# A hybrid transformer step on one core: splitting the experts' weight tiles in halves of 1024 columns

## The chip, the cores and the metric

The kernel runs on one core of a Trainium2 chip. The metric is the time of one execution on the device in microseconds (us). The engines are TensorE (PE, matmuls; its weight loads are shown apart as PEld), VectorE (DVE), ScalarE (ACT), GpSimd (POOL) and SyncE (SP), whose queue issues nearly all loads here. Each engine runs its own list of instructions; they are held together by semaphores, counters that an instruction raises as it ends and on which another waits.

## The reference

Two token sets (256 prompt tokens and 8 x 4 sample tokens, model width 1024) go through two layers: the first has a sparse attention mixer and a dense feed-forward, the second a short convolution and a mixture of 8 experts, of which every token uses 2. All weights are fp32. The change is in the experts:

```python
def _moe(h, w_router, b_router, w_gu, w_down):
    logits = (h @ w_router).astype(jnp.float32) + b_router.astype(jnp.float32)
    top_v, top_i = lax.top_k(logits, TOP_K)
    top_w = jax.nn.softmax(top_v, axis=-1)
    combine = jnp.sum(jax.nn.one_hot(top_i, N_EXPERTS, dtype=jnp.float32) * top_w[..., None], axis=-2).astype(h.dtype)
    out = jnp.zeros_like(h)
    for e in range(N_EXPERTS):
        out = out + combine[..., e:e + 1] * _swiglu(h, w_gu[e], w_down[e])
    return out
```

`_swiglu` is `(silu(h @ w_gate) * (h @ w_up)) @ w_down` with a hidden width of 3584.

## The kernel before

All weights and cache pages stream through one ring of six slots in SBUF (`ring`, 128 partitions x 2048 columns of fp32, 1 MB each). SP issues the loads in the order of use. Before it loads tile n it waits until the tile six places earlier is used (`s_used`, L491 and, in the experts, L505).

Matmuls with fp32 weights of the ada, dense, conv and expert stages are done in three fast matmuls. ACT copies a tile into a buffer of type fp32r, which rounds it (`whi` in the experts, L757), DVE subtracts this high part from the tile (`wlo`, L1307), and PE multiplies high by high, low by high and high by low. Three semaphores carry a tile through. ACT raises `s_split_hi`. DVE waits for that, and raises `s_used`, which frees the ring slot and at the same time tells PE that both parts are there. PE raises `s_tile_done` with its last matmul on the tile, and ACT waits for that before it overwrites the split buffer. The experts have three split buffers (`SPLIT`), so ACT may copy tile i when PE is done with tile i-3.

The expert loop runs eight times on each engine (`experts`, L502 on SP, L751 on ACT, L1297 on DVE, L1796 on PE), for one expert each. Further rounds for over 128 tokens at one expert are in the code, and weren't entered here. An expert has 42 tiles. The first 28 hold gate and up weights: a tile is 4 row blocks of 512 columns, and each block is used in three matmuls (L1835 to L1837). The last 14 hold the down weights: a tile is 2 row blocks of 1024 columns, with six matmuls each (L1856). Ahead of the tiles PE gathers the expert's tokens by matmuls with a selection matrix (L1803, recorded on the helper's line L1358) and DVE and ACT split the gathered rows (`XTh`, `XTl`, L761 and L1312). Every four tiles ACT computes a silu (L768), DVE multiplies (L1322), PE transposes the product (`turn`, L1819), and ACT and DVE split it (L772, L1327). Behind the tiles ACT and DVE copy the result from PSUM (L775, L1330), PE scatters it to the tokens (L1864) and DVE adds it up (L1333).

The same three semaphores count on through the stages before the experts: 48 ada tiles (L593, L798, L1398), 42 dense tiles (L600, L1150, L1694) and 16 conv tiles (L607, L1182, L1763). The attention stages free their slots with increments by PE.

On the instruction streams, the matter of the change reads like this:

```python
# ACT, L756
a.wait_ge(s_tile_done, e * TILES_E + (SPLIT_AT_M + i + 1 - SPLIT))
a.activation(whi[:, i % SPLIT, :], ring[:, (T_MOE + i) % RING, :], ACT.Copy).then_inc(s_split_hi, 1)
# DVE, L1306
v.wait_ge(s_split_hi, e * TILES_E + (SPLIT_AT_M + i + 1))
v.tensor_tensor(wlo[:, i % SPLIT, :], ring[:, (T_MOE + i) % RING, :],
                whi[:, i % SPLIT, :].bitcast(F32), ALU.subtract).then_inc(s_used, 1)
# PE, L1812
pe.wait_ge(s_used, e * TILES_E + (T_MOE + i + 1))
```

Of the kernel before, what the change touches and what calls it, by code (L numbers as in the profile page):

```python
# [30 lines left out]
NE = 8  # L31
# [6 lines left out]
RING = 6  # L38
# [3 lines left out]
SPLIT = 3  # L42
SPLIT_F = 2
# [34 lines left out]
def trunk(nc, A, O):  # L78
    with ExitStack() as ctx:
# [395 lines left out]
        def _(sp):  # L475
            sp.dma_start(pgt[:], A["page_table"].rearrange("(o b) p -> o (b p)", o=1)).then_inc(s_pages_in, 16)
            for n, ent in enumerate(stream):
                if n == T_CACHE:
                    sp.wait_ge(s_pages_in, 16)
                if isinstance(ent, tuple) and ent[0] == "page":  # L480
                    _, kind, b, kv = ent
                    src = A["cache_cmp_kv"] if kind == "cmp" else A["cache_sel_kv"]
                    for j in range(8):
                        pg = sp.value_load(pgt[0:1, b * 8 + j:b * 8 + j + 1], min_val=0, max_val=src.shape[1] - 1)  # L484
                        if j == 0:
                            sp.wait_ge(s_used, n - RING + 1)
# [3 lines left out]
                if n >= RING:  # L490
                    sp.wait_ge(s_used, n - RING + 1)  # L491
# [76 lines left out]
        def _(a):  # L568
# [19 lines left out]
            def ada_hi(i):  # L588

                wait_tile(a, i)  # L590
                if i >= SPLIT:
                    a.wait_ge(s_tile_done, i - SPLIT + 1)
                a.activation(ahi[:, i % SPLIT, :], ring[:, i % RING, :], ACT.Copy).then_inc(s_split_hi, 1)  # L593

            def ffn_hi(i):

                wait_tile(a, T_FU + i)
                if i >= SPLIT_F:
                    a.wait_ge(s_tile_done, SPLIT_AT_F + i - SPLIT_F + 1)
                a.activation(fhi[:, i % SPLIT_F, :], ring[:, (T_FU + i) % RING, :], ACT.Copy).then_inc(s_split_hi, 1)  # L600

            def conv_hi(i):

                wait_tile(a, T_CI + i)
                if i >= SPLIT_F:
                    a.wait_ge(s_tile_done, SPLIT_AT_C + i - SPLIT_F + 1)
                a.activation(chi[:, i % SPLIT_F, :], ring[:, (T_CI + i) % RING, :], ACT.Copy).then_inc(s_split_hi, 1)  # L607
# [118 lines left out]
            for i in range(1, TILES_F):  # L726
                ffn_hi(i)
                if i < 28 and i % 4 == 3:
                    j = i // 4
                    a.wait_ge(s_tile_done, SPLIT_AT_F + 4 * j + 2)  # L730
# [7 lines left out]
            for i in range(1, TILES_C):  # L738
                conv_hi(i)
                k = (i - 3) // 2  # L740
                if i % 2 == 1 and k in (0, 1, 3, 4):
                    wh, jt = k % 3, k // 3
                    a.wait_ge(s_tile_done, SPLIT_AT_C + 2 * k + 2)
# [7 lines left out]
            def experts(rnd):  # L751
                with a.Fori(0, NE) as e0:
                    e = e0 + NE * rnd
                    for i in range(TILES_E):
                        wait_expert_tile(a, e, i)
                        a.wait_ge(s_tile_done, e * TILES_E + (SPLIT_AT_M + i + 1 - SPLIT))  # L756
                        a.activation(whi[:, i % SPLIT, :], ring[:, (T_MOE + i) % RING, :], ACT.Copy).then_inc(s_split_hi, 1)  # L757
# [5 lines left out]
                        if i % 4 == 2 and 6 <= i <= 30:  # L763
                            j = (i - 6) // 4
                            a.wait_ge(s_tile_done, e * TILES_E + (SPLIT_AT_M + 4 * j + 4))
# [8 lines left out]
                    a.wait_ge(s_tile_done, e * TILES_E + (SPLIT_AT_M + TILES_E))  # L774
# [12 lines left out]
        def _(v):  # L787
# [30 lines left out]
            for k in range(24):  # L818
# [3 lines left out]
                v.wait_ge(s_tile_done, 2 * k + 2)  # L822
# [324 lines left out]
            def ffn_lo(i):  # L1147

                v.wait_ge(s_split_hi, SPLIT_AT_F + i + 1)
                v.tensor_tensor(flo[:, i % SPLIT_F, :], ring[:, (T_FU + i) % RING, :], fhi[:, i % SPLIT_F, :].bitcast(F32),  # L1150
                                ALU.subtract).then_inc(s_used, 1)

            v.wait_ge(s_used, T_FU)
# [6 lines left out]
            for i in range(1, TILES_F):  # L1160
                ffn_lo(i)
                if i % 4 == 1 and 5 <= i <= 29:
# [3 lines left out]
                    v.wait_ge(s_tile_done, SPLIT_AT_F + 4 * j + 4)  # L1166
# [6 lines left out]
            def from_dn(c):  # L1173
                v.wait_ge(s_tile_done, SPLIT_AT_F + 28 + 7 * (c // 4 + 1))
# [4 lines left out]
            def conv_lo(i):  # L1179

                v.wait_ge(s_split_hi, SPLIT_AT_C + i + 1)
                v.tensor_tensor(clo[:, i % SPLIT_F, :], ring[:, (T_CI + i) % RING, :], chi[:, i % SPLIT_F, :].bitcast(F32),  # L1182
                                ALU.subtract).then_inc(s_used, 1)
# [12 lines left out]
            for c in range(DC):  # L1196
# [4 lines left out]
                v.wait_ge(s_tile_done, SPLIT_AT_C + 2 * k + 2)  # L1201
# [29 lines left out]
            def from_co(c):  # L1231
                v.wait_ge(s_tile_done, SPLIT_AT_C + 12 + 2 * (c // 4) + 2)
# [64 lines left out]
            def experts(rnd):  # L1297
# [5 lines left out]
                with v.Fori(0, NE) as e0:  # L1303
                    e = e0 + NE * rnd
                    for i in range(TILES_E):
                        v.wait_ge(s_split_hi, e * TILES_E + (SPLIT_AT_M + i + 1))  # L1306
                        v.tensor_tensor(wlo[:, i % SPLIT, :], ring[:, (T_MOE + i) % RING, :],  # L1307
                                        whi[:, i % SPLIT, :].bitcast(F32), ALU.subtract).then_inc(s_used, 1)
# [20 lines left out]
                    v.wait_ge(s_tile_done, e * TILES_E + (SPLIT_AT_M + TILES_E))  # L1329
# [24 lines left out]
        def _(pe):  # L1354
# [34 lines left out]
            for k in range(24):  # L1389
# [3 lines left out]
                for kc in range(8):  # L1393
                    i = n + kc // 4
                    if kc % 4 == 0:
                        pe.wait_ge(s_used, i + 1)
# [4 lines left out]
                    if kc % 4 == 3:  # L1401
                        ins.then_inc(s_tile_done, 1)
# [557 lines left out]
```

## Time and profile before

| | |
|---|---|
| median of three runs | 2338.59 us (2336.14 to 2339.79) |
| the profiled execution's own time | 2335.71 us |
| its span, first to last instruction | 2333.9 us |
| mean granted clock of TensorE | 0.943 of full |
| busy, share of the span | PE 90%, PEld 69%, DVE 64%, ACT 47%, POOL 1% |
| loads | 537.62 MB, mean 230 GB/s |

All rows come from the one profiled execution. A busy share says how much an engine did, not who made the others wait; for that there are views of waits (an engine's idle time, put down to what ended it) and of the chain of work that ended last. In a timeline, a row begins with the start and the length in us; the difference of two starts is the pitch at which an engine moves on, which may be shorter than one instruction's length, since they overlap.

### The profile page before, as it was taken

What the parts mean: (1) busy time and instruction counts of PE and PEld (TensorE: products, weight loads), DVE (VectorE), ACT (ScalarE), POOL (GpSimd) and SP (SyncE); (2) the same over time, 40 slices, a digit from 0 to 9 for tenths busy, and PEclk for the clock granted to TensorE, in tenths of its full rate; (3) what the DMA queues carried; (4) which work ended last, traced back from release to release, by engine and by line L of the source; (5) the groups of instructions that cost most, each with busy time, mean ns of one, the idle gap of its engine ahead of it and who ended that gap; (6) DMA issues with size and microseconds to landing.
All of it is one profiled execution on the core that took longest, in us unless ns stands there. A gap on an engine that the chain in (4) does not pass through costs nothing.

```text
span 2333.9 us, 29561 instructions
## 1 busy us (share of the span) xinstructions
PE 2097.2 (90%) x10775; PEld 1619.7 (69%) x10775; DVE 1484.8 (64%) x1684; ACT 1091.2 (47%) x961; POOL 14.9 (1%) x26
## 2 busy tenths in 40 slices
PE   5989899869747899998869999999999999999995
PEld 2443355445535799997868878787887878788783
DVE  5981221166522544435667879788887979788885
ACT  4750020024311333324235767576676757576671
POOL 0000010000000000000000000000000000000000
PEclk9999999957978999998978999999999999999997
DMA  9984343200357665443317979798997979899890
GB/s 315 382 318 108 88 137 115 93 0 1 108 167 196 246 204 163 167 158 127 127 38 274 371 280 377 280 362 323 326 374 282 376 276 372 310 339 362 285 362 22
DMA packets 262788, 537.62 MB, mean 230 GB/s; under 512 B 14876, under 2 KB 56068, under 8 KB 262438
## 3 DMA queue, kind: packets, MB, share of 16 engines
q1 hardware_dynamic: 258514, 520.34, 63.5%
q0 software_dynamic: 1984, 13.45, 1.7%
q10 hardware_dynamic: 2196, 2.61, 0.3%
q8 instruction: 56, 0.92, 0.2%
q14 instruction: 38, 0.31, 0.0%
HBM read 533.32 MB, written 11.35 MB: 233 GB/s over the span
## 4 chain that ended last, share of the span: by engine, by line
PE 81%; DVE 7%; SPq 3%; issue 3%; ACT 2%; DMA 2%; ACTq 1%; POOL 0%; DVEq 0%; PEldq 0%
PE ps L1358 19%; PE ps L1856 13%; PE ps L1835 9%; PE ps L1837 9%; PE ps L1836 9%; PE ps L1694 5%; PE ps L1696 5%; PE ps L1695 5%; DVE alo L798 2%; DMA ring<-in_w_ada 2%; SPq L484 2%; SPq L487 1%; PE ps L1574 1%; PE ps L1486 1%; PE ps L1819 1%
## 5 line engine op out<-in xcount | busy, mean ns | idle before, releaser
L1307 DVE TENSOR_TENSOR wlo<-ring,whi 128x2048 fp32r<-128x2048 f32 x336 | 767.2, 2291 | 117.9 <-ACT whi L757 117.9
L757 ACT ACTIVATE whi<-ring 128x2048 fp32r<-128x2048 f32 x336 | 642.1, 1918 | 233.0 <-PE ps L1837 166.4
L1835 PE MATMUL ps<-whi,XTh 128*128 128x512 f32 x896 | 355.1, 396 | 0.0
L1837 PE MATMUL ps<-whi,XTl 128*128 128x512 f32 x896 | 350.0, 391 | 0.0
L1836 PE MATMUL ps<-wlo,XTh 128*128 128x512 f32 x896 | 349.4, 390 | 0.0
L1835 PEld LDWEIGHTS ps<-whi,XTh 128*128 128x128 f32 x896 | 168.7, 188 | 36.1 <-DVE wlo L1307 2.5
L1837 PEld LDWEIGHTS ps<-whi,XTl 128*128 128x128 f32 x896 | 168.5, 188 | 35.8
L1836 PEld LDWEIGHTS ps<-wlo,XTh 128*128 128x128 f32 x896 | 168.9, 188 | 33.6
L1150 DVE TENSOR_TENSOR flo<-ring,fhi 128x2048 fp32r<-128x2048 f32 x42 | 96.3, 2292 | 137.9 <-ACT fhi L600 137.9
L600 ACT ACTIVATE fhi<-ring 128x2048 fp32r<-128x2048 f32 x42 | 80.6, 1920 | 174.5 <-PE ps L1696 169.5
L1694 PE MATMUL ps<-hTh,fhi 128*128 128x288 f32 x448 | 132.8, 296 | 10.3 <-DVE hTl L1159 10.3
L1856 PE MATMUL ps<-whi,actTh 128*128 128x512 f32 x448 | 139.5, 392 | 0.0
L1856 PE MATMUL ps<-wlo,actTh 128*128 128x512 f32 x448 | 138.2, 390 | 0.0
L1856 PE MATMUL ps<-whi,actTl 128*128 128x512 f32 x448 | 138.1, 389 | 0.0
L1696 PE MATMUL ps<-hTh,flo 128*128 128x288 f32 x448 | 132.9, 297 | 0.0
L1695 PE MATMUL ps<-hTl,fhi 128*128 128x288 f32 x448 | 132.7, 296 | 0.0
L1358 PE MATMUL ps<-ring,hT 128*128 128x512 f32 (+3 forms) x288 | 111.7, 546 | 9.3 <-ACT hT L632 7.4
L1358 PE MATMUL ps<-work 128*128 128x273 f32 (+1 forms) x256 | 115.4, 625 | 3.5 <-DVE work L947 3.5
L798 DVE TENSOR_TENSOR alo<-ring,ahi 128x2048 fp32r<-128x2048 f32 x48 | 108.4, 2283 | 10.9 <-ACT ahi L593 10.3
L947 DVE COPY work<-ps 128x512 f32<-128x512 f32 x56 | 38.4, 691 | 116.2 <-PE ps L1486 104.2
L665 ACT ACTIVATE work<-ps 128x512 f32<-128x512 f32 x56 | 33.4, 597 | 166.2 <-PE ps L1486 105.5
L593 ACT ACTIVATE ahi<-ring 128x2048 fp32r<-128x2048 f32 x48 | 90.8, 1915 | 36.0 <-PE ps L1399 23.8
(321 smaller groups left out, 3166.1 us busy)
## 6 DMA issues: line engine op xcount, KB each, us to landing
ring<-in_w_moe_gu SPq DMA_DIRECT2D x224, 1024.0 KB, 6.9
ring<-in_w_moe_down SPq DMA_DIRECT2D x112, 1024.0 KB, 6.7
ring<-in_w_ada SPq DMA_DIRECT2D x48, 1024.0 KB, 10.4
ring<-in_w_ff_gu SPq DMA_DIRECT2D x28, 1024.0 KB, 5.4
ring<-in_cache_cmp_kv SPq DMA_DIRECT2D x128, 128.0 KB, 2.1
ring<-in_cache_sel_kv SPq DMA_DIRECT2D x128, 128.0 KB, 2.2
ring<-in_w_ff_down SPq DMA_DIRECT2D x14, 1024.0 KB, 5.0
ring<-in_w_conv_in SPq DMA_DIRECT2D x12, 1024.0 KB, 5.2
```

The costliest lines, as they stand in the source:

```text
L757: a.activation(whi[:, i % SPLIT, :], ring[:, (T_MOE + i) % RING, :], ACT.Copy).then_inc(s_split_hi, 1)
L798: v.tensor_tensor(alo[:, i % SPLIT, :], ring[:, i % RING, :], ahi[:, i % SPLIT, :].bitcast(F32), ALU.subtract).then_inc(s_used, 1)
L1150: v.tensor_tensor(flo[:, i % SPLIT_F, :], ring[:, (T_FU + i) % RING, :], fhi[:, i % SPLIT_F, :].bitcast(F32), ALU.subtract).then_inc(s_use ...
L1307: v.tensor_tensor(wlo[:, i % SPLIT, :], ring[:, (T_MOE + i) % RING, :], whi[:, i % SPLIT, :].bitcast(F32), ALU.subtract).then_inc(s_used, 1)
L1358: return pe.matmul(out, l, r, start=(k == 0), stop=(k == n - 1), **kw)
L1694: pe.matmul(out, hi, xh, start=first, stop=False)
L1695: pe.matmul(out, hi, xl, start=False, stop=False)
L1696: return pe.matmul(out, lo, xh, start=False, stop=last)
L1835: pe.matmul(out, XTh[:, kc, :], hi, start=kc == 0, stop=False)
L1836: pe.matmul(out, XTh[:, kc, :], lo, start=False, stop=False)
L1837: ins = pe.matmul(out, XTl[:, kc, :], hi, start=False, stop=kc == 7)
L1856: ins = pe.matmul(ps[:, 6 + h, :], a_[:, k, :], w_[:, kk, 512 * h:512 * h + 512], start=first and k == 0, stop=last and k == 27)
```

## The change

In the expert loop each tile is split in two halves of 1024 columns (`HALF`). ACT copies a half and raises `s_split_hi` for it, having waited until PE is done with the same half of tile i-3. DVE subtracts a half and raises `s_used` for it. PE waits for each half (two row blocks of a gate or up tile, one of a down tile) and raises `s_tile_done` after each. The ring slot is still freed as a whole: SP waits until both halves are used. Since the counters run on from the earlier stages, every other increment of the three semaphores becomes 2, and every value waited for is doubled.

```diff
+HALF = SLOT // 2
...
                     for i in range(TILES_E):
-                        sp.wait_ge(s_used, (e + NE * rnd) * TILES_E + (T_MOE + i - RING + 1))
+                        sp.wait_ge(s_used, (e + NE * rnd) * (2 * TILES_E) + 2 * (T_MOE + i - RING + 1))
...
                 if i >= SPLIT:
-                    a.wait_ge(s_tile_done, i - SPLIT + 1)
-                a.activation(ahi[:, i % SPLIT, :], ring[:, i % RING, :], ACT.Copy).then_inc(s_split_hi, 1)
+                    a.wait_ge(s_tile_done, 2 * (i - SPLIT + 1))
+                a.activation(ahi[:, i % SPLIT, :], ring[:, i % RING, :], ACT.Copy).then_inc(s_split_hi, 2)
...
                         wait_expert_tile(a, e, i)
-                        a.wait_ge(s_tile_done, e * TILES_E + (SPLIT_AT_M + i + 1 - SPLIT))
-                        a.activation(whi[:, i % SPLIT, :], ring[:, (T_MOE + i) % RING, :], ACT.Copy).then_inc(s_split_hi, 1)
+                        for p in range(2):
+                            c0 = HALF * p
+                            a.wait_ge(s_tile_done, e * (2 * TILES_E) + (2 * (SPLIT_AT_M + i - SPLIT) + p + 1))
+                            a.activation(whi[:, i % SPLIT, c0:c0 + HALF], ring[:, (T_MOE + i) % RING, c0:c0 + HALF], ACT.Copy
+                                         ).then_inc(s_split_hi, 1)
...
-                v.wait_ge(s_split_hi, i + 1)
+                v.wait_ge(s_split_hi, 2 * (i + 1))
                 v.tensor_tensor(alo[:, i % SPLIT, :], ring[:, i % RING, :], ahi[:, i % SPLIT, :].bitcast(F32),
-                                ALU.subtract).then_inc(s_used, 1)
+                                ALU.subtract).then_inc(s_used, 2)
...
-                        v.wait_ge(s_split_hi, e * TILES_E + (SPLIT_AT_M + i + 1))
-                        v.tensor_tensor(wlo[:, i % SPLIT, :], ring[:, (T_MOE + i) % RING, :],
-                                        whi[:, i % SPLIT, :].bitcast(F32), ALU.subtract).then_inc(s_used, 1)
+                        for p in range(2):
+                            c0 = HALF * p
+                            v.wait_ge(s_split_hi, e * (2 * TILES_E) + (2 * (SPLIT_AT_M + i) + p + 1))
+                            v.tensor_tensor(wlo[:, i % SPLIT, c0:c0 + HALF], ring[:, (T_MOE + i) % RING, c0:c0 + HALF],
+                                            whi[:, i % SPLIT, c0:c0 + HALF].bitcast(F32), ALU.subtract).then_inc(s_used, 1)
...
-                    def split_wait(i):
+                    def split_wait(i, p):
 
-                        pe.wait_ge(s_used, e * TILES_E + (T_MOE + i + 1))
+                        pe.wait_ge(s_used, e * (2 * TILES_E) + (2 * (T_MOE + i) + p + 1))
...
-                                if kc % 4 == 0:
-                                    split_wait(i)
+                                if kc % 2 == 0:
+                                    split_wait(i, kc % 4 // 2)
...
-                                if kc % 4 == 3:
+                                if kc % 2 == 1:
                                     ins.then_inc(s_tile_done, 1)
...
-                        split_wait(28 + i)
...
                             k = 2 * i + kk
+                            split_wait(28 + i, kk)
...
-                        ins.then_inc(s_tile_done, 1)
+                            ins.then_inc(s_tile_done, 1)
```

The dense and conv stages change as the ada lines do, and PE's own increments of `s_used` and `s_tile_done` in all earlier stages are doubled.

## Rows read from the trace of the kernel before

**Rows 1.** The page's head: busy share of each engine, and the chain by engine.

```profile
PE 2097.2 (90%) x10775; PEld 1619.7 (69%) x10775; DVE 1484.8 (64%) x1684; ACT 1091.2 (47%) x961; POOL 14.9 (1%) x26
...
PE 81%; DVE 7%; SPq 3%; issue 3%; ACT 2%; DMA 2%; ACTq 1%; POOL 0%; DVEq 0%; PEldq 0%
```

**Rows 2.** Stretches (us): length; busy PE, PEld, DVE, ACT, POOL; granted clock; DMA share; GB/s.

```profile
790.00:1060.00 270.00, 262.95 (x1969) 261.17 (x1967) 125.08 (x93) 92.23 (x62) 0.00 (x0) 0.99 0.52 175
...
1240.00:2300.00 1060.00, 1039.77 (x4737) 848.38 (x4735) 883.79 (x608) 723.63 (x483) 0.00 (x0) 1.00 0.89 324
...
1490.40:1623.40 133.00, 131.13 (x600) 106.97 (x599) 111.53 (x77) 91.40 (x61) 0.00 (x0) 1.00 0.90 327
```

**Rows 3.** Waits, 1240 to 2300 us: total, times, longest.

```profile
PEld ps L1358 <- ACT nT L775: 10.1, 8, 1.3
PEld ps L1835 <- DVE wlo L1307: 2.5, 8, 0.3
...
ACT whi L757 <- PE ps L1837: 166.4, 208, 4.7
...
SPq L516 <- DVE wlo L1307: 837.9, 327, 17.5
```

**Rows 4.** Timeline of PE over a tile's edge: start, length, instruction.

```profile
1301.10 0.39 PE L1837 MATMUL ps<-whi,XTl 128*128 128x512 f32 x1
...
1303.82 0.39 PE L1837 MATMUL ps<-whi,XTl 128*128 128x512 f32 x1
1304.04 0.39 PE L1835 MATMUL ps<-whi,XTh 128*128 128x512 f32 x1
```

**Rows 5.** Timelines of ACT and DVE in the loop.

```profile
1263.84 0.59 ACT L772 ACTIVATE actTh<-ps 128x512 fp32r<-128x512 f32 x1
...
1301.52 1.92 ACT L757 ACTIVATE whi<-ring 128x2048 fp32r<-128x2048 f32 x1 [0.80 <-PE ps L1837]
...
1492.42 5.51 ACT L757 ACTIVATE whi<-ring 128x2048 fp32r<-128x2048 f32 x3
...
1265.70 0.68 DVE L1322 TENSOR_TENSOR actM<-siluM,ps 128x512 f32<-128x512 f32 x1
1266.30 0.68 DVE L1327 TENSOR_TENSOR actTl<-ps,actTh 128x512 fp32r<-128x512 f32 x1
...
1303.47 2.29 DVE L1307 TENSOR_TENSOR wlo<-ring,whi 128x2048 fp32r<-128x2048 f32 x1 [0.21 <-ACT whi L757]
...
1496.49 6.70 DVE L1307 TENSOR_TENSOR wlo<-ring,whi 128x2048 fp32r<-128x2048 f32 x3 [0.53 <-ACT whi L757]
```

**Rows 6.** Timeline of PE at the wait for wlo in the second expert.

```profile
1391.32 0.39 PE L1837 MATMUL ps<-whi,XTl 128*128 128x512 f32 x1
...
1391.94 0.39 PE L1836 MATMUL ps<-wlo,XTh 128*128 128x512 f32 x1
```

**Rows 7.** Timelines of DVE and PE at the seam between experts.

```profile
1490.52 0.69 DVE L1330 COPY nT<-ps 128x512 f32<-128x512 f32 x1 [3.92 <-PE ps L1856]
...
1503.11 0.68 DVE L1312 TENSOR_TENSOR XTl<-ps,XTh 128x512 fp32r<-128x512 f32 x1
...
1491.35 0.72 PE L1358 MATMUL ps<-nT 128*128 128x288 f32 x2 [0.88 <-DVE nT L1330]
...
1505.44 0.50 PE L1835 MATMUL ps<-whi,XTh 128*128 128x512 f32 x1
```

**Rows 8.** PE's wait line: register operations, ns least/median/most.

```profile
L1812 PEldq ALU_OP  x328: 32/32/42, 1236.9 to 2282.4; - x164
```

**Rows 9.** The chain that ended last, in order of time, in the ada stage.

```profile
104.12 11.43 DMA ring<-in_w_ada
```

**Rows 10.** Load queues, 1400 to 2200 us; DVE's timeline behind the loop.

```profile
q1 hardware_dynamic: 111840, 264.85, 90.7%
...
2298.50 0.48 DVE L864 SCALAR_TENSOR_TENSOR xT<-hT,modT,xT 128x256 f32<-128x256 f32 x1 [4.13 <-issue]
...
2301.06 0.19 DVE L866 TENSOR_TENSOR small<-hT,modT 128x32 f32<-128x32 f32 x1 [1.35 <-issue]
```

More of the change, by code:

```diff
@@ L490, in _ @@
                 if n >= RING:
-                    sp.wait_ge(s_used, n - RING + 1)
+                    sp.wait_ge(s_used, 2 * (n - RING + 1))
                 if isinstance(ent, tuple):
@@ L598, in ffn_hi @@
                 if i >= SPLIT_F:
-                    a.wait_ge(s_tile_done, SPLIT_AT_F + i - SPLIT_F + 1)
-                a.activation(fhi[:, i % SPLIT_F, :], ring[:, (T_FU + i) % RING, :], ACT.Copy).then_inc(s_split_hi, 1)
+                    a.wait_ge(s_tile_done, 2 * (SPLIT_AT_F + i - SPLIT_F + 1))
+                a.activation(fhi[:, i % SPLIT_F, :], ring[:, (T_FU + i) % RING, :], ACT.Copy).then_inc(s_split_hi, 2)
             def conv_hi(i):
@@ L605, in conv_hi @@
                 if i >= SPLIT_F:
-                    a.wait_ge(s_tile_done, SPLIT_AT_C + i - SPLIT_F + 1)
-                a.activation(chi[:, i % SPLIT_F, :], ring[:, (T_CI + i) % RING, :], ACT.Copy).then_inc(s_split_hi, 1)
+                    a.wait_ge(s_tile_done, 2 * (SPLIT_AT_C + i - SPLIT_F + 1))
+                a.activation(chi[:, i % SPLIT_F, :], ring[:, (T_CI + i) % RING, :], ACT.Copy).then_inc(s_split_hi, 2)
             def norm(n):
@@ L729, in _ @@
                     j = i // 4
-                    a.wait_ge(s_tile_done, SPLIT_AT_F + 4 * j + 2)
+                    a.wait_ge(s_tile_done, 2 * (SPLIT_AT_F + 4 * j + 2))
                     if j >= 2:
@@ L742, in _ @@
                     wh, jt = k % 3, k // 3
-                    a.wait_ge(s_tile_done, SPLIT_AT_C + 2 * k + 2)
+                    a.wait_ge(s_tile_done, 2 * (SPLIT_AT_C + 2 * k + 2))
                     b0 = 4 * (k % 2)
@@ L821, in _ @@
                         ada_lo(i)
-                v.wait_ge(s_tile_done, 2 * k + 2)
+                v.wait_ge(s_tile_done, 2 * (2 * k + 2))
                 if k >= 2:
@@ L1147, in ffn_lo @@
             def ffn_lo(i):
-                v.wait_ge(s_split_hi, SPLIT_AT_F + i + 1)
+                v.wait_ge(s_split_hi, 2 * (SPLIT_AT_F + i + 1))
                 v.tensor_tensor(flo[:, i % SPLIT_F, :], ring[:, (T_FU + i) % RING, :], fhi[:, i % SPLIT_F, :].bitcast(F32),
-                                ALU.subtract).then_inc(s_used, 1)
-            v.wait_ge(s_used, T_FU)
+                                ALU.subtract).then_inc(s_used, 2)
+            v.wait_ge(s_used, 2 * T_FU)
             ffn_lo(0)
@@ L1173, in from_dn @@
             def from_dn(c):
-                v.wait_ge(s_tile_done, SPLIT_AT_F + 28 + 7 * (c // 4 + 1))
+                v.wait_ge(s_tile_done, 2 * (SPLIT_AT_F + 28 + 7 * (c // 4 + 1)))
                 return ps[:, c, :]
@@ L1179, in conv_lo @@
             def conv_lo(i):
-                v.wait_ge(s_split_hi, SPLIT_AT_C + i + 1)
+                v.wait_ge(s_split_hi, 2 * (SPLIT_AT_C + i + 1))
                 v.tensor_tensor(clo[:, i % SPLIT_F, :], ring[:, (T_CI + i) % RING, :], chi[:, i % SPLIT_F, :].bitcast(F32),
-                                ALU.subtract).then_inc(s_used, 1)
+                                ALU.subtract).then_inc(s_used, 2)
             conv_lo(0)
@@ L1395, in _ @@
                     if kc % 4 == 0:
-                        pe.wait_ge(s_used, i + 1)
+                        pe.wait_ge(s_used, 2 * (i + 1))
                     c0 = 512 * (kc % 4)
@@ L1401, in _ @@
                     if kc % 4 == 3:
-                        ins.then_inc(s_tile_done, 1)
+                        ins.then_inc(s_tile_done, 2)
                 if k:
@@ L1438, in _ @@
                         if t == 2 and kc == 3 and not last:
-                            ins.then_inc(s_used, 1)
+                            ins.then_inc(s_used, 2)
                 ins.then_inc(s_proj_done, 1)
                 pe.wait_ge(s_proj_done, ct + 1)
-                pe.sem_inc(s_used, 1)
+                pe.sem_inc(s_used, 2)
             cols = [128 * i for i in range(8)] + [1536, 1664, 2048, 2176, 1024, 1152, 1280, 1408]
@@ L1489, in _ @@
                         pe.wait_ge(s_bank_turned, jb[0])
-                        pe.sem_inc(s_used, 1)
+                        pe.sem_inc(s_used, 2)
                     copied()
@@ L1592, in turn_keys @@
                     pe.wait_ge(s_bank_turned, jb[0])
-                    pe.sem_inc(s_used, 1)
+                    pe.sem_inc(s_used, 2)
             def turn_out(tau):
@@ L1658, in _ @@
                 pe.wait_ge(s_group_pv, tau + 1)
-                pe.sem_inc(s_used, 3)
+                pe.sem_inc(s_used, 6)
             turn_out(3)
@@ L1672, in dense @@
                         if b == 3 and kc == 3:
-                            ins.then_inc(s_used, 1)
+                            ins.then_inc(s_used, 2)
                     ins.then_inc(done, 1)
@@ L1676, in dense @@
                 pe.wait_ge(done, nd[done])
-                pe.sem_inc(s_used, 1)
+                pe.sem_inc(s_used, 2)
             nd = {}
@@ L1704, in _ @@
                 j, u, half = i // 4, (i // 2) % 2, i % 2
-                pe.wait_ge(s_used, T_FU + i + 1)
+                pe.wait_ge(s_used, 2 * (T_FU + i + 1))
                 if j and half == 0:
@@ L1714, in _ @@
                                        kc == 0, kc == 7)
-                ins.then_inc(s_tile_done, 1)
+                ins.then_inc(s_tile_done, 2)
             for ch in range(2):
@@ L1719, in _ @@
                     t = 28 + 7 * ch + i
-                    pe.wait_ge(s_used, T_FU + t + 1)
+                    pe.wait_ge(s_used, 2 * (T_FU + t + 1))
                     if ch == 0:
@@ L1727, in _ @@
                                            m == 0, m == 27)
-                    ins.then_inc(s_tile_done, 1)
+                    ins.then_inc(s_tile_done, 2)
             norm(2)
@@ L1745, in _ @@
                     pe.wait_ge(s_tail_rows, 2)
-                pe.wait_ge(s_used, T_CI + i + 1)
+                pe.wait_ge(s_used, 2 * (T_CI + i + 1))
                 if k == 1 and half == 0:
@@ L1764, in _ @@
                                        kc == 0, kc == 7)
-                ins.then_inc(s_tile_done, 1)
+                ins.then_inc(s_tile_done, 2)
             norm(3)
```

15 lines of the change are left out of this document (7 added, 8 removed).

## The prediction

> **What bounds the kernel now.** Three views, in this order. The page's head says what is long: TensorE (PE) is busy for 90% of the span, and four fifths of the chain that ended last is PE [rows 1]. A share of the whole span hides stages, so the second view is the table of stretches. Between 1240 and 2300 us, 45% of the span, lie the eight experts, whose tiles the change cuts; there PE is busy for 1039.8 of 1060 us at the full granted clock of 1.00 (2.4 GHz), VectorE (DVE) for 883.8 and ScalarE (ACT) for 723.6 [rows 2]. The third view is who waited for whom in that stretch [rows 3]. It decides the case. ACT waits for PE 166.4 us: it copies a tile as soon as a split buffer is given back, and then rests. The queue that issues the loads waits for DVE 837.9 us, so no load is late. PE's own weight loads wait 10.1 us at the seams between experts, for the copy of the result out of PSUM, which the change leaves alone. For the split weights, which the change hands over earlier, they wait 2.5 us, eight times 0.3.
>
> The sum of one expert closes without any other idle time. The second expert's stretch is 133.0 us [rows 2]. A tile is 12 matmuls at a pitch of 0.2267 us (1303.82 less 1301.10 is 2.72 us for twelve, over a tile's edge [rows 4]), and 42 tiles make 114.2 us. The rest is seven turns of the activations, the seam and the gather ahead of the next expert. So a tile costs what its matmuls cost, and the split is ready before PE asks for it.
>
> **The change, part by part.** *Earlier hand-over.* Before, tile i may be copied when tile i-3 is wholly used; PE wants it two tiles later, 5.44 us. The chain between is ACT 1.92 + DVE 2.29 us [rows 5], with some 0.03 us at each hand-over (ACT's copy ends at 1303.44, DVE starts at 1303.47): about 4.3 us, a slack of 1.1. After, a first half is given back 1.36 us earlier and its chain is about 1.04 + 1.22 + 0.1 = 2.4 us (half the columns off 1.92 and 2.29, at the pitches below), against 6.8: a slack of 4.4. Slack that is not used is worth nothing; the gain is the waits that there are. They lie once in each expert, where ACT loads a table for the silu: PE takes 0.62 us there for two matmuls (1391.32 to 1391.94 [rows 6]). Against two pitches of 0.227 that is 0.17 us, and 8 x 0.17 = 1.4 us. The row of waits bounds the gain at 2.5 [rows 3], and 0 is the other end: an earlier hand-over makes nobody wait. I take 1.4.
>
> *Twice the instructions on ACT and DVE.* 336 copies and 336 subtractions become 672 each. The trace has no such instruction of 1024 columns, so I draw a line through two that it has. On DVE, three in a row of 2048 columns take 6.70 us and the last 2.29, a pitch of (6.70 - 2.29) / 2 = 2.205; one of 512 columns from PSUM has 0.60 (1265.70 to 1266.30) [rows 5]. The line gives 1.135 for 1024, so two halves take 2.27, 0.065 more than one whole. Ends: 0 (the halves together as the whole) and 0.2 (four times 0.60 less 2.205). On ACT a whole has a pitch of (5.51 - 1.92) / 2 = 1.795, and a copy of 512 columns is 0.59 long; four of those, 2.36, bound the two halves from above, 1.795 from below. I take a twentieth above the whole, 1.88, as on DVE nearer to the lower end. The cover is PE's pace: four tiles take 4 x 2.72 = 10.9 us, with four of them DVE has two shorter steps, 4 x 2.27 + 2 x 0.60 = 10.3 us of work (10.8 at the upper end), and ACT at most 4 x 2.36 + 2 x 0.59 = 10.6. Were the cover gone, the price would be 336 x 0.065 = 22 us. At the seam DVE makes three tiles between its last addition and the split of the gathered rows; that split ends at 1503.79 and PE starts on it at 1505.44 [rows 7]: 3 x 0.065 = 0.2 us (at most 0.6) goes into 1.65 us of room. Path cost 0.
>
> *Twice the waits and releases on PE.* Each expert gets 42 more waits on its weight loads, each with a register operation on PE's sequencer (32 ns, one for nearly every wait before [rows 8]), and 42 more increments on matmuls. At a tile's edge both stand already: the matmul of 1303.82 increments, the weight load behind it waits, and the next start follows at 1304.04, after 0.22, no more than the mean pitch [rows 4]. So 0. Queued behind each new wait are the tile's remaining matmuls, and behind those the next half that ACT may overwrite; as the slack grows, the wait is met when it is read. In the down projection the wait moves from tile to half tile, ahead of the wait for the turned activations: same order, nothing overtaken.
>
> The Trainium skill has a rule against this part: "TensorE: Matmul & The Clock Gate", section "The cost: per-tile semaphore tail", charges 26.3 ns for every increment beyond the first at the end of packed matmuls. By it 336 more increments would cost an estimated 8.8 us. The trace disagrees so far: the edge above shows none of it.
>
> *The load queue.* It waits for whole tiles as before. A ring slot is freed when DVE's second half ends, about 1.9 us sooner relative to PE (1.92 + 2.29 against about 2.3). The loads could start sooner, but no one waits for them. 0.
>
> *Counters that step by 2 everywhere else.* The ada, dense and conv stages keep whole tiles and add 2 to the shared counters. No row shows an instruction that adds 2 as it ends; the nearest are the hand-overs just read, which add 1. Should the wait then have to stand as an instruction of its own, the nearest row is PE's start behind DVE's copy at the seam: the copy ends at 1491.21, the matmul starts at 1491.35, 0.14 us against 0.03 [rows 7]. In the ada stage the ring's chain is load, ACT, DVE, next load, with the load the longest [rows 9]: 48 tiles in 6 slots are 8 rounds, and 8 x 3 x 0.11 = 2.6 us; in the dense stage PE is busy for 263 of 270 us [rows 2] and covers it. So 0 to 2.6 us, no gain. I take 0, because the loads dominate that chain (11.43 us of each round) and a hand-over that adds 1 within the instruction is the nearest row.
>
> *Code.* The loop bodies get longer, so what follows lies elsewhere in memory, and a stop for the next piece of code, such as the 1.35 us on DVE after the loop [rows 10], can come or go: 1.4 us either way.
>
> Sum: -1.4 + 0 + 0 + 0 = -1.4 us against the profiled execution's own 2335.7. The median of the runs is 2338.6, 2.9 above that, and goes down by as much: 2337.2.
>
> **The rivals.** *Slower by code loading.* ACT's and DVE's bodies get 42 more instructions each, and register operations for their waits. Now the loop runs without loading: from 1400 to 2200 us only the data queue moves [rows 10]. If the longer bodies no longer stay loaded, every jump back costs what a jump to unloaded code costs: DVE was idle for 4.13 us on leaving the loop [rows 10]. At the seam 1.65 us of that is covered; the rest, 2.5 us, falls on each of seven jumps back, with DVE's 0.2 about 19 us: 2356. It decides as soon as one body exceeds what is kept. Against it: PE's far longer body stays loaded too. The Trainium skill, "Advanced Engine Details and Errata", section "ISA Cache", gives each engine a store of two pieces of 256 instructions (TensorE four times that). By that page 84 more instructions beside bodies of a few times 42 would still fit, as an estimate, and this rival would not happen; no run so far shows the limit.
>
> *Slower by PE's sequencer.* If an added register operation or increment is not hidden, its price is 32 ns x 336 = 10.8 us: 2348. It decides only where PE's sequencer has no matmul queued. Against it stands the tile's edge [rows 4].
>
> *Faster, because the pitch shrinks.* 512 columns at 2.4 GHz are 0.213 us, PE's pitch is 0.227. If the 13 ns came from whole tiles being written beside PE's reads, halves might give some back: 4032 matmuls x 13 ns = 54 us at most, half of it 27: 2311. Against it stands the dense stage: there ACT and DVE write for a third and under half of the time, and PE's 263 us over 1969 matmuls, nearly all of 288 columns, are 0.134 us each, against 0.120 at 2.4 GHz [rows 2]. The excess is the same with fewer writes beside it.
>
> **How the numbers follow.** The forecast, nothing on the path, gets 0.82; code loading 0.06, PE's sequencer 0.05, a shorter pitch 0.03, and 0.04 is left for what I don't see. About 0.2%, 4.7 us, is what a measurement of this kernel can tell from no change; the forecast lies within it. The range of the forecast: downwards 2.5 in place of 1.4, 1.4 for code and the 2.5 by which the lowest run lies under the median give 2332.3; upwards no gain, 2.6 for counters, 1.4 for code and the 1.2 of the highest run give 2343.8. The slower rivals stay outside, within the 2 in 10. Faster: 0.03 plus a tail of the forecast, 0.07; slower: 0.11 plus a tail, 0.14; the same 0.79.
>
> **What would show it.** Right: PE's pitch of 0.227 and an expert of 133 us unchanged; the 2.5 us of waits for wlo gone; ACT's and DVE's busy time up by some 28 and 22 us (336 x 0.085 and 0.065); DVE's idle ahead of wlo split over twice the count. Wrong: an instruction queue at work inside the loop, a pitch over 0.227 at a half tile's edge, new waits of PE for wlo, or longer ada rounds. The prediction falls if an expert's stretch moves by over 0.5 us.

## The result, and the profile after

The changed kernel takes 2344.59 us (median of six runs, 2342.63 to 2347.89), the kernel before 2336.68 (six runs, 2334.05 to 2339.79). The ratio is 1.0035 [1.0023, 1.0048]: slower by about 8 us. The forecast was "the same" and 2337.2 (-1.4 us, counted down from 2338.6), with an upper end of 2343.8.

The page of the changed kernel, as far as it answers to [rows 1]: each engine's busy time, the chain by engine, and the two groups that were split (busy and mean ns of one; idle time ahead of them and what ended most of it).

```profile
PE 2109.0 (90%) x10775; PEld 1633.0 (70%) x10775; DVE 1523.2 (65%) x2020; ACT 1149.6 (49%) x1297; POOL 14.9 (1%) x26
...
PE 81%; DVE 7%; SPq 4%; issue 3%; ACT 2%; DMA 2%; ACTq 1%; DVEq 0%; POOL 0%; PEldq 0%
...
L1313 DVE TENSOR_TENSOR wlo<-ring,whi 128x1024 fp32r<-128x1024 f32 x672 | 805.8, 1222 | 61.2 <-ACT whi L760 11.6
L760 ACT ACTIVATE whi<-ring 128x1024 fp32r<-128x1024 f32 x672 | 706.2, 1060 | 170.8 <-PE ps L1843 120.9
```

The two groups in the kernel before:

```profile
L1307 DVE TENSOR_TENSOR wlo<-ring,whi 128x2048 fp32r<-128x2048 f32 x336 | 767.2, 2291 | 117.9 <-ACT whi L757 117.9
L757 ACT ACTIVATE whi<-ring 128x2048 fp32r<-128x2048 f32 x336 | 642.1, 1918 | 233.0 <-PE ps L1837 166.4
```

The chain is nearly as it was. PE executes the same number of matmuls as before, yet is busy 11.8 us longer. To see where, I took PE's jump back at the end of each expert and cut the loop at these points. The columns are those of [rows 2]: stretch, length, busy times, then the granted clock. First the kernel before, from the end of the first expert to the end of the eighth, and its seventh expert alone:

```profile
1362.90:2294.50 931.60, 918.33 (x4193) 748.96 (x4193) 780.72 (x539) 634.87 (x425) 0.00 (x0) 1.00 0.89 324
...
2028.40:2161.40 133.00, 131.14 (x599) 107.02 (x599) 111.53 (x77) 91.40 (x63) 0.00 (x0) 1.00 0.91 331
```

Then the changed kernel, the same seven experts together, and the last three of them one by one:

```profile
1364.30:2302.00 937.70, 924.56 (x4193) 754.97 (x4193) 814.54 (x833) 686.38 (x717) 0.00 (x0) 0.99 0.88 322
...
1895.90:2028.70 132.80, 130.94 (x599) 107.10 (x599) 116.33 (x119) 98.74 (x104) 0.00 (x0) 1.00 0.90 332
2028.70:2169.10 140.40, 138.56 (x599) 112.56 (x599) 116.50 (x119) 98.72 (x104) 0.00 (x0) 0.94 0.85 314
2169.10:2302.00 132.90, 131.00 (x599) 107.08 (x599) 116.34 (x119) 93.83 (x99) 0.00 (x0) 1.00 0.78 284
```

Of the seven, six take 132.8 to 132.9 us, about 0.2 less than before. That is the gain of the forecast. One takes 140.4, and only there is the mean granted clock 0.94. The page's row of the clock, in tenths over 40 equal slices of the span, shows the same at a glance (before, then changed): the loop fills the slices behind the 22nd but for the last, and there the changed kernel has one 8, in the 35th.

```profile
PEclk9999999957978999998978999999999999999997
...
PEclk9999989957878999998968999999999999899997
```

PE's timeline at the seam ahead of that expert, with the seam before it for comparison (start, length, instruction, in brackets the idle time before it). The row with x16 scatters an expert's result, the one with x48 gathers the next expert's tokens; an fp32 matmul of the program stands in the profile as two instructions, so these are 8 and 24 matmuls:

```profile
1891.15 4.12 PE L1364 MATMUL ps<-nT 128*128 128x288 f32 x16 [0.88 <-DVE nT L1336]
...
1896.26 8.51 PE L1364 MATMUL ps<-nT,hN 128*128 128x128 f32 x48 [0.98 <-DVE hT L1339]
...
2023.96 4.12 PE L1364 MATMUL ps<-nT 128*128 128x288 f32 x16 [0.88 <-DVE nT L1336]
2029.07 13.41 PE L1364 MATMUL ps<-nT,hN 128*128 128x128 f32 x48 [0.99 <-DVE hT L1339]
...
2043.86 0.63 PE L1842 MATMUL ps<-wlo,XTh 128*128 128x512 f32 x1
2044.29 0.63 PE L1843 MATMUL ps<-whi,XTl 128*128 128x512 f32 x1
...
2048.65 0.39 PE L1842 MATMUL ps<-wlo,XTh 128*128 128x512 f32 x1
2048.88 0.39 PE L1843 MATMUL ps<-whi,XTl 128*128 128x512 f32 x1
```

Both seams have the same idle times, 0.88 and 0.98 or 0.99 us. In the second one the granted clock falls to half (1.2 GHz) at 2031.2, inside the gather, which takes 13.41 us in place of 8.51. The first tile's matmuls follow it at a pitch of 0.43 us. At 2048.2 the clock is full again and the pitch 0.23. This costs 7.5 us (140.4 less 132.9). The profiled execution is 9.0 us longer than that of before (2344.71 against 2335.71): 6.1 us inside the seven experts (937.7 less 931.6, which is 7.5 lost and 1.4 gained), 1.4 ahead of the first expert's end and 1.5 behind the eighth's (40.9 us to the end of the span against 39.4). The traces of the experiments below give no sign that the last two come from the halves. The router's first matmul starts at 1199.2 us before and 1200.4 in the changed kernel, but at 1199.7 and 1198.0 in two runs with halves (the filled seam and the seams shifted back), and anywhere from 1198.4 to 1202.8 in five runs with whole tiles. From the start of the last scatter to the end of the span it is 44.1 us before, 45.7 in the changed kernel, and 43.3 and 44.1 in the same two runs with halves.

On PE's path all else in the loop is as forecast. The waits of PE's weight loads, 1245 to 2300 us (total, times, longest), name no split weights any more; the 2.5 us of [rows 3] are gone. (Of the 18 pauses put down to "issue", 12 lie around the one gather at half clock.)

```profile
PEld ps L1364 <- issue: 12.6, 18, 1.5
PEld ps L1364 <- ACT nT L779: 10.1, 8, 1.3
PEld ps L1813 <- issue: 1.6, 8, 0.3
```

PE's timeline over two edges of half tiles that follow each other, one of them inside a tile, where the increment and the wait are new, has the pitch of [rows 4]; a tile of twelve matmuls is 2 x 1.36 = 2.72 us as before:

```profile
1302.47 0.39 PE L1843 MATMUL ps<-whi,XTl 128*128 128x512 f32 x1
1302.70 0.39 PE L1841 MATMUL ps<-whi,XTh 128*128 128x512 f32 x1
...
1303.83 0.39 PE L1843 MATMUL ps<-whi,XTl 128*128 128x512 f32 x1
1304.06 0.39 PE L1841 MATMUL ps<-whi,XTh 128*128 128x512 f32 x1
```

### The profile page after: what moved, and what is told of

Its sections match the earlier page's. It is cut to its first block, busy times and chain, and to the rows that moved or that the text cites. A ratio compares the mean times of both kernels' runs of the same rounds, so it can differ in the third digit from the quotient of the medians.

```text
span 2342.9 us, 31350 instructions
## 1 busy us (share of the span) xinstructions
PE 2109.0 (90%) x10775; PEld 1633.0 (70%) x10775; DVE 1523.2 (65%) x2020; ACT 1149.6 (49%) x1297; POOL 14.9 (1%) x26
## 4 chain that ended last, share of the span: by engine, by line
PE 81%; DVE 7%; SPq 4%; issue 3%; ACT 2%; DMA 2%; ACTq 1%; DVEq 0%; POOL 0%; PEldq 0%
PE ps L1364 19%; PE ps L1862 13%; PE ps L1841 9%; PE ps L1843 9%; PE ps L1842 9%; PE ps L1700 5%; PE ps L1702 5%; PE ps L1701 5%; DVE alo L802 2%; SPq L485 2%; SPq L488 2%; PE ps L1580 1%; PE ps L1492 1%; PE ps L1825 1%; DMA ring<-in_w_ada 1%
## 5 line engine op out<-in xcount | busy, mean ns | idle before, releaser
L1313 DVE TENSOR_TENSOR wlo<-ring,whi 128x1024 fp32r<-128x1024 f32 x672 | 805.8, 1222 | 61.2 <-ACT whi L760 11.6
L760 ACT ACTIVATE whi<-ring 128x1024 fp32r<-128x1024 f32 x672 | 706.2, 1060 | 170.8 <-PE ps L1843 120.9
L1702 PE MATMUL ps<-hTh,flo 128*128 128x288 f32 x448 | 132.8, 296 | 0.0
## 6 DMA issues: line engine op xcount, KB each, us to landing
ring<-in_w_ada SPq DMA_DIRECT2D x48, 1024.0 KB, 10.1
```

The lines of the kernel that those rows point to most:

```text
L760: a.activation(whi[:, i % SPLIT, c0:c0 + HALF], ring[:, (T_MOE + i) % RING, c0:c0 + HALF], ACT.Copy).then_inc(s_split_hi, 1)
L1313: v.tensor_tensor(wlo[:, i % SPLIT, c0:c0 + HALF], ring[:, (T_MOE + i) % RING, c0:c0 + HALF], whi[:, i % SPLIT, c0:c0 + HALF].bitcast(F32) ...
L1702: return pe.matmul(out, lo, xh, start=False, stop=last)
```

## The experiments

The change moves a seam's work nowhere; it only moves the time at which a seam comes, 0.2 us earlier for each expert that went by, 1.1 us by the sixth seam counted from the first. So the first theory was: the granted clock falls at a seam if that comes at an unlucky time, and the change shifts one there. Its rivals: the halves themselves, with more instructions of ACT and DVE beside PE, bring the fall about; or the counters that step by 2 cost something. Extra matmuls stand in as a lever: they have the identity as one operand and write to a PSUM bank that is free.

**Counters by 2 alone.** The kernel before, whole tiles, all steps and waited values of the three counters doubled.

```diff
-                            a.wait_ge(s_tile_done, e * TILES_E + (SPLIT_AT_M + i + 1 - SPLIT))
-                            a.activation(whi[:, i % SPLIT, :], ring[:, (T_MOE + i) % RING, :], ACT.Copy).then_inc(s_split_hi, 1)
+                            a.wait_ge(s_tile_done, e * (2 * TILES_E) + 2 * (SPLIT_AT_M + i + 1 - SPLIT))
+                            a.activation(whi[:, i % SPLIT, :], ring[:, (T_MOE + i) % RING, :], ACT.Copy).then_inc(s_split_hi, 2)
...
```

> The kernel before with whole tiles, but every counter stepping by 2 as in the change. Theory (the loss is one fall of TensorE's clock at a seam between two experts, some 7.5 us, which comes because the halves shorten each expert by 0.19 us and so move the seams): counters alone leave the expert period at 133.07 us, no fall inside the loop, ratio to before 1.000 within 0.001. Rival (the loss comes from the doubled counters in the stages ahead of the experts, where the changed kernel's conv stage was 2.6 us longer): ratio 1.002 to 1.004, conv stage or ada rounds longer.

Measured: 2335.65 us, 1.0008 [0.9997, 1.0019]. Its second expert, in the columns of [rows 2]:

```profile
1362.60:1495.80 133.20, 131.30 (x599) 106.99 (x599) 111.54 (x77) 91.40 (x63) 0.00 (x0) 1.00 0.90 331
```

The clock stays at 1.00 through the loop (932.1 us from the first scatter to the last, against 931.6), an expert has its old length within 0.1 us, and the router's first matmul, at 1198.4 us, is no later than before. The counters don't make the 0.35%; a cost of their own of up to 0.19% isn't excluded.

**The seam filled, with halves.** The changed kernel, and at each seam one fp32 matmul of 512 columns ahead of the wait for the result's copy and one ahead of the wait for the last addition, where PE rests.

```diff
+                    mm(ps[:, 5, :], ident, con[:, 0:512], 0, 1)
                     pe.wait_ge(s_y_act, e + 1)
...
+                    mm(ps[:, 5, :], ident, con[:, 0:512], 0, 1)
                     pe.wait_ge(s_share_added, e * 8 + 8)
```

> The changed kernel with two extra matmuls of 512 fp32 columns (some 0.85 us each) at every seam, in PE's two idle gaps there (1.26 us ahead of the scatter, 1.39 us ahead of the gather); their product is never read. Theory (clock at the seam): PE is busier at the seam, the clock stays up at all seven seams inside the loop, every expert takes 132.9 us, time about 2336 us, ratio to before 0.998 to 1.001, against 1.0035 for the change without them. Rival (halves themselves slow a stage): no effect, ratio stays at 1.0035.

Measured: 2333.67 us, 0.9993 [0.9984, 1.0002]. The seventh expert, the clock over the span, and PE's timeline at the seam ahead of that expert (the expectation counts the idle gaps from the start of the last matmul, the timelines above from its end):

```profile
2028.20:2161.10 132.90, 132.75 (x604) 107.81 (x603) 116.36 (x119) 98.78 (x105) 0.00 (x0) 1.00 0.90 331
...
PEclk9999989957968999998978999999999999999997
...
2022.25 1.02 PE L1364 MATMUL ps<-con 128*128 128x512 f32 x2
2023.29 4.12 PE L1364 MATMUL ps<-nT 128*128 128x288 f32 x16
2027.24 1.02 PE L1364 MATMUL ps<-con 128*128 128x512 f32 x2
2028.39 8.51 PE L1364 MATMUL ps<-nT,hN 128*128 128x128 f32 x48
```

The fillers cover the idle 0.88 and 0.99 us and prolong nothing; the gather has its 8.51 us and the clock stays at 1.00. With no other edit the whole loss is gone. Nor did the fillers move this seam to a better time: its gather starts 805.8 us after the start of the first gather in both traces (2028.39 less 1222.64 here, 2029.07 less 1223.31 in the changed kernel). The halves need not lose; at the same time of the seam, it is the rest in it that lets the clock fall.

**The seam filled, with whole tiles.** The same two matmuls in the kernel before.

> The kernel before with the same two extra matmuls at every seam. Theory: before had no fall at the seams in its profiled execution, so nothing is to be gained there, and the matmuls fit the gaps: ratio 1.000 within 0.001. If falls also come in some executions of before, the spread of its times shrinks. Rival (extra matmuls cost time at the seam): 8 times up to 0.9 us, ratio up to 1.003.

Measured: 2334.15 us, 0.9996 [0.9986, 1.0007]; the second expert:

```profile
1362.50:1495.60 133.10, 132.91 (x604) 107.75 (x603) 111.53 (x77) 91.40 (x62) 0.00 (x0) 1.00 0.91 331
```

Nothing was to be won there, since the kernel before loses no clock at its seams. Against the run above, halves are 0.2 us shorter an expert.

**Whole tiles, seams 0.25 us later per expert.** The kernel before, with one matmul of 174 columns in each expert, in the dense run of the gate and up tiles. The shift goes the other way, but no tile is cut.

```diff
+                        if j == 3:
+                            mm(ps[:, 7, 0:174], ident, con[:, 0:174], 0, 1)
                         if j:
                             turn(j - 1)
```

> The kernel before, whole tiles, with one extra matmul of 174 fp32 columns (some 0.29 us) in the middle of each expert, away from the seam; its product is never read. Theory (what decides is when a seam comes, not the halves): the expert period goes to 133.36 us, the seams move against the clock's grid by as much as in the change but the other way, and a fall at some seam comes in many executions: 2.3 us for the matmuls, plus 7.5 us where it comes, ratio 1.001 without and 1.004 with it; its profile shows a low clock in the gather of one expert. Rival (halves slow it): 2.3 us and nothing else, ratio 1.001, no fall.

Measured: 2340.95 us (2338.65 to 2344.79), 1.003 [1.0018, 1.0042]. The seventh and the eighth expert, and PE's timeline at the seam between:

```profile
2030.00:2163.30 133.30, 131.45 (x601) 107.32 (x601) 111.60 (x77) 91.37 (x62) 0.00 (x0) 1.00 0.91 330
2163.30:2304.20 140.90, 138.96 (x601) 112.71 (x601) 111.61 (x77) 86.36 (x58) 0.00 (x0) 0.94 0.73 268
...
2163.55 13.09 PE L1358 MATMUL ps<-nT,hN 128*128 128x128 f32 x48 [0.99 <-DVE hT L1333]
```

The extra work is 8 x 0.25 = 2 us; the loss was 6 to 7. The same fall, in the same instructions, in a kernel without any half tile: the clock falls in the gather at the seventh seam, 7 x 0.25 = 1.75 us later than in the kernel before. So the halves are not what it takes. In the six runs the mean clock was 0.932 twice (2344.4 and 2344.8 us) and 0.937 or 0.938 four times (2338.7 to 2341.2): here the fall may come in some executions only, but one alone was looked at in a trace, and the four are still 4.0 to 6.6 us over the median of before, more than the 2 us of added work, so this is not settled.

**Halves, seams shifted back.** The changed kernel, with one such matmul of 112 columns, to make an expert as long as it was before.

```diff
+                        if j == 3:
+                            mm(ps[:, 7, 0:112], ident, con[:, 0:112], 0, 1)
```

> The changed kernel with one extra matmul of 112 fp32 columns (some 0.19 us) in the middle of each expert, away from the seam; its product is never read. It gives each expert the length that it had before the change. Theory (when the seams come decides): the expert period is 133.07 us again, no fall of the clock inside the loop, 8 x 0.19 = 1.5 us are paid and some 7.5 us saved against the change; ratio to before 0.999 to 1.002. Rival (the halves bring the fall at the seam, whenever it comes): ratio 1.004, a fall in the profile.

Measured: 2336.21 us, 1.0003 [0.9993, 1.0013]; the second expert, and the clock over the span:

```profile
1361.60:1494.70 133.10, 131.21 (x601) 107.33 (x601) 116.47 (x119) 98.87 (x104) 0.00 (x0) 1.00 0.91 331
...
PEclk9999999957978999998978999999999999999997
```

Eight matmuls more than the changed kernel, and the loss is gone: no seam has a fall, the gathers at all seven take 8.51 us. This and the run before it are the two sides of one test, and both go with the time of the seam.

**Whole tiles, larger shifts.** If the time decides, further shifts should bring falls at other seams, and some none. The kernel before with two matmuls of 270 columns in an expert (0.9 us), and with two of 360 (1.2 us).

```diff
+                        if j == 3:
+                            for _ in range(2):
+                                mm(ps[:, 7, 0:270], ident, con[:, 0:270], 0, 1)
```

> The kernel before, whole tiles, with two extra matmuls of 270 fp32 columns (together some 0.9 us) in the middle of each expert, away from the seam. Theory, worked out from which seams fell and which did not in the four profiles so far: the third seam and the sixth come where the clock falls; 7.2 us for the matmuls and 7.5 us for each fall, two falls 22 us, ratio 1.0095 (one fall 1.006). Rival (a fall has nothing to do with when the seams come): 7.2 us, ratio 1.003.

Measured: 2358.16 us, 1.0104 [1.0085, 1.0124]. Experts two to four, and the sixth:

```profile
1365.00:1499.00 134.00, 132.07 (x603) 107.76 (x603) 111.63 (x77) 91.44 (x63) 0.00 (x0) 1.00 0.91 329
1499.00:1640.50 141.50, 139.60 (x603) 113.27 (x603) 111.63 (x77) 91.44 (x63) 0.00 (x0) 0.94 0.86 311
1640.50:1774.40 133.90, 132.08 (x603) 107.76 (x603) 111.63 (x77) 91.33 (x62) 0.00 (x0) 1.00 0.90 329
...
1908.40:2049.90 141.50, 139.62 (x603) 113.20 (x603) 111.63 (x77) 91.43 (x62) 0.00 (x0) 0.94 0.85 311
```

Two falls, as forecast, but at the second and the fifth seam, not at the third and the sixth. The number came out and the place did not, so the rule by which I placed them is not exact, and that their number was right is in part luck.

> The kernel before, whole tiles, with two extra matmuls of 360 fp32 columns (together some 1.2 us) in the middle of each expert, away from the seam. Theory, from the same four profiles: no seam comes where the clock falls; 9.6 us for the matmuls and nothing else, ratio 1.004, so less time lost than with the shorter matmuls of 0.9 us. Rival (the longer the expert, the more is lost): more than with 0.9 us.

Measured: 2343.8 us, 1.0043 [1.0028, 1.0059]. The seven experts behind the first:

```profile
1368.00:2307.70 939.70, 926.72 (x4221) 754.16 (x4221) 781.41 (x539) 634.99 (x425) 0.00 (x0) 1.00 0.88 321
```

The longer extra work makes the faster kernel: 14 us less than with 0.9 us per expert. No seam has a fall, and what is left is the 8 x 1.2 = 9.6 us of added matmuls. A cost that grew with the work could not do this.

**A version that beats both.** The gather ahead of the first expert is at half clock in the kernel before too; it takes 15.06 us where later gathers take 8.51. Its stretch, and that gather:

```profile
1190.00:1245.00 55.00, 39.05 (x172) 32.27 (x171) 30.03 (x79) 16.66 (x20) 0.00 (x0) 0.63 0.17 58
...
1221.87 15.06 PE L1358 MATMUL ps<-nT,hN 128*128 128x128 f32 x48 [8.54 <-DVE nT L1294]
```

So I filled, besides the seams of the changed kernel, the long stops of PE around the loop: 7 matmuls ahead of the wait for the normalised tokens of the router, 9 ahead of the wait that precedes the first gather, 6 ahead of the last norm and 10 behind it.

```diff
             norm(3)
+            for _ in range(7):
+                mm(ps[:, 5, :], ident, con[:, 0:512], 0, 1)
             h_ready(3)
...
+            for _ in range(9):
+                mm(ps[:, 6, :], ident, con[:, 0:512], 0, 1)
             pe.wait_ge(s_rows_taken, 6)
...
+            for _ in range(6):
+                mm(ps[:, 7, :], ident, con[:, 0:512], 0, 1)
             norm(4)
+            for _ in range(10):
+                mm(ps[:, 7, :], ident, con[:, 0:512], 0, 1)
             pe.wait_ge(s_final_ready, 1)
```

> The changed kernel with extra matmuls of 512 fp32 columns, whose product is never read, in PE's idle times: two at each seam as before, and seven ahead of the router, nine ahead of the first gather, six and ten around the last norm. If the clock is what PE's idle times cost, these stages run at the full clock: the first gather 9 us for 15, the router and the turning of the tokens some 3 us less, the end some 4 us less; about 2323 us, ratio 0.994 to 0.996. If the matmuls come too late or fill more than the idle time: ratio 0.999 or over.

Measured: 2324.66 us (2323.66 to 2336.36), 0.9956 [0.9939, 0.9973]. The profiled execution was the one of 2336.36, so it tells little of the others. In it the gather ahead of the first expert still took 13.01 us, so the fillers did not hold the clock there, and the six matmuls ahead of the last norm began only after a stop of PE of 9.40 us for which the profile names no wait, and pushed the norm back.

```profile
2302.56 6.86 PE L1364 MATMUL ps<-con 128*128 128x512 f32 x12 [9.40 <-issue]
```

Without these six:

> The changed kernel with extra matmuls as in the run before (two at each seam, seven ahead of the router, nine ahead of the first gather, ten ahead of the last turning), but without the six ahead of the last norm, which began only after PE's 9.4 us stop behind the loop and so pushed the norm back. Theory: 3 to 5 us less than with the six, about 2321 us, ratio 0.993 to 0.996.

Measured: 2325.15 us (2320.53 to 2325.63), 0.9958 [0.9944, 0.9972]. The ratio is that of the run with the six, so the 3 to 5 us expected from leaving them out did not come; what they cost in most executions isn't known. The stretch ahead of the loop, and its gather, against 0.63 and 15.06 us above:

```profile
1190.00:1245.00 55.00, 52.86 (x263) 38.56 (x262) 40.98 (x98) 25.39 (x33) 0.00 (x0) 0.97 0.28 98
...
1222.91 8.51 PE L1364 MATMUL ps<-nT,hN 128*128 128x128 f32 x48 [0.71 <-DVE nT L1298]
```

And the same fillers in the kernel with whole tiles:

> The kernel before, whole tiles, with the same extra matmuls. With the clock held up in the loop in both, what is left between this and the last is what the halves bring by themselves. Theory (they take away 0.19 us in each expert): 1.5 us more than the last, about 2322.5 us. Rival (halves cost something of their own, in the loop or by the steps of 2 ahead of it): 1 to 3 us less than the last.

Measured: 2325.07 us, 0.9964 [0.995, 0.9978]; the eight experts:

```profile
1245.00:2290.00 1045.00, 1039.68 (x4710) 842.96 (x4708) 873.89 (x599) 714.00 (x477) 0.00 (x0) 1.00 0.89 326
```

Both beat the kernel before by 0.4%, and they differ by 0.1 us. Once the clock is held, the halves bring nothing that these runs can measure; the 1.5 us of the theory lie within their scatter, and the rival's cost of 1 to 3 us doesn't show either.

## Why the prediction was wrong

*The step that failed* is the reading of [rows 2]. "Busy for 1039.8 of 1060 us at the full granted clock of 1.00" was taken as a property of the loop, and the sum priced the change by waits and instructions alone. It was a property of the seven seams between the experts as they happened to be timed. The idle time at each seam stood in [rows 3] (10.1 us) and [rows 7]; I called it a thing "which the change leaves alone" and didn't ask what the clock does there if it comes at another time. No rival had a fall at a seam: the 7.5 us it costs in the profiled execution are more than the range's whole distance from forecast to upper end (6.6). The prediction's own sign of falling came: one expert's stretch moved by over 0.5 us, to 140.4 from 133.0. With the rest in the seams filled, the changed kernel ran 1.0 us under the kernel before (2333.67 against 2334.67), near the forecast's -1.4: the term that was missing is the clock. The stretch ahead of the loop could have warned me: there the same gather already ran at half clock.

*Earlier hand-over, -1.4 us.* Right. The waits for the split weights are gone, experts without a fall are 0.2 us shorter (0.17 forecast), and the seven gain 7.5 - 6.1 = 1.4. This gain is also what set off the loss: a kernel with halves and the old length of an expert has none.

*ACT and DVE.* On the path 0, right; the busy time was undersized, and DVE's idle time ahead of its subtractions was not split over twice the count but fell from 117.9 to 61.2 us. DVE's busy time went up by 38.6 us (805.8 against 767.2) where 22 stood, ACT's by 64 (706.2 against 642.1) where 28 stood. The pitch in a row of several was sized well:

```profile
1493.59 5.79 ACT L760 ACTIVATE whi<-ring 128x1024 fp32r<-128x1024 f32 x6
...
1497.68 3.50 DVE L1313 TENSOR_TENSOR wlo<-ring,whi 128x1024 fp32r<-128x1024 f32 x3 [0.56 <-ACT whi L760]
```

Two of ACT take (5.79 - 1.06) / 5 x 2 = 1.89 us (1.88 forecast) and DVE's pitch is (3.50 - 1.22) / 2 = 1.14 (1.135). But most halves run singly, behind a pause, and then the full length counts: 2 x 1.060 against 1.92 on ACT, 2 x 1.222 against 2.29 on DVE. I had priced by pitch what waits had pulled apart.

*Twice the waits and releases on PE.* 0, right: the edges above keep the pitch. By the rule of the Trainium skill cited in the prediction ("TensorE: Matmul & The Clock Gate", "The cost: per-tile semaphore tail") an expert would have become an estimated 42 x 26.3 ns = 1.1 us longer; six became 0.2 us shorter, so no run here shows such a cost.

*Load queue and code.* In the loop right: nobody waits for a load, and from 1400 to 2200 us again only the data queue moves, so the longer bodies stay loaded and the rival of code loading falls. Behind the loop DVE's two stops of 4.13 and 1.35 us [rows 10] became one of 7.52, 2.0 us more in all, where I gave 1.4 to code. The path doesn't feel it: with the seams shifted back DVE stops there for 7.72 us, and the end comes as long after the last scatter as in the kernel before (44.1 us).

```profile
q1 hardware_dynamic: 110705, 262.59, 89.4%
...
2309.38 0.48 DVE L868 SCALAR_TENSOR_TENSOR xT<-hT,modT,xT 128x256 f32<-128x256 f32 x1 [7.52 <-issue]
```

*Counters by 2.* 0 to 2.6 us was forecast; measured alone they are -0.03 to +0.19%, up to 4.4 us. Not told apart from 0.

*The shorter pitch* was rightly given little: no matmul became faster. (Its 54 us are 4032 x 13.4 ns; 13 is rounded.)

## What to carry to other kernels

A full granted clock in the profile is a state of that execution's timing and no constant of a stage: where a dense stage has short idle seams, price a fall at one of them (here 7.5 us) as a rival of every change that shifts them, even one that only saves time. Before a small loss is put down to the edit, look at the granted clock part by part, and make the test of the two sides: the edit with the old timing, and the old code with the new timing. A few matmuls whose result nobody reads, laid into PE's stops, can be worth more than the saving itself; look in the trace whether they begin when the stop does, since those placed ahead of the last norm began late and pushed it back in the execution that was looked at.

## What the runs showed of the hardware

The clock fell at a seam where PE had rested only twice, for 0.88 and 0.99 us, around small fp32 matmuls; other seams of the same make, in the same execution, did not fall. In all four falls that I looked at (one in the changed kernel, one and two with 0.25 and 0.9 us more per expert) it was the gather behind the second rest that slowed down, and an expert became 7.5 us longer. Counted from the start of the first gather, and beside the seam of the same number in the kernel before, the gather with a fall came 1.2 us earlier in the changed kernel (805.8 us against 806.9), 1.8 us later with 0.25 more per expert (941.8 against 939.9), and with 0.9 more 1.7 us later (276.3 against 274.6) and, behind its first fall, 11.8 later (685.7 against 673.9). Seams 1.25 and 2.5 us later (the first two with 1.2 more) had none. It is not a matter of more or less idle time, which was equal. Why just these times, what else the chip weighs, and why the changed kernel was longer in each of its runs and not in some, stays open: that a fall goes with the seam's time was shown, the mechanism behind it was not.
